# A gated ConvFFN in four token groups: down tiles issued between the next group's up blocks

## What is computed

```python
def conv_ffn(h, past, w_up, w_conv, b_conv, w_down):
    up = h @ w_up
    full = jnp.concatenate([past.astype(up.dtype), up], axis=1)
    conv = b_conv + full[:, 0:t] * w_conv[0]
    for k in range(1, CONV_W):
        conv = conv + full[:, k:k + t] * w_conv[k]
    gate, val = jnp.split(conv, 2, axis=-1)
    return (jax.nn.gelu(gate) * val) @ w_down, full[:, t:]
...
    x = x + gate_f * f
...
y_prompt = rms_norm(xp, final_g)
```

## Time and profile before

| | us |
|---|---|
| median of 2 runs | 1898.5 (1896.73 to 1900.27) |
| the profiled execution | 1895.18 |
| its span, slowest of 8 cores | 1893.5 |
| span of the other cores | 1873.4 to 1892.7 |
| TensorE busy over the span | 61% |
| VectorE, ScalarE, GpSimd busy | 49%, 32%, 27% |
| granted TensorE clock, mean | 0.828 on this core |

### The profile page before, as it was taken

The page is one execution under the profiler, slowest core; times in us unless marked ns, Lnnn a source line. Parts: engine busy times, 40 slices in busy tenths (PEclk is TensorE's granted clock), DMA queues, the critical chain, the costliest instruction groups (busy, mean ns, idle before and its releaser), DMA issues.

```text
span 1893.5 us, 26226 instructions; the slowest of 8 cores (1873.4 to 1893.5 us)
## 1 busy us (share of the span) xinstructions
PE 1147.3 (61%) x6276; PEld 584.0 (31%) x6276; DVE 920.6 (49%) x2237; ACT 610.8 (32%) x1104; POOL 513.6 (27%) x464
## 2 busy tenths in 40 slices
PE   0020554236244318659999885789897577886493
PEld 0020443123122103324444442333343233333241
DVE  0057516741555404534444364778623588885031
ACT  0010003651144406733333253445412244442012
POOL 0056511120000003431110363555412244442011
PEclk9999955558566658979999797999998788898797
DMA  6155982322300170044431774997523244448922
GB/s 26 20 53 51 94 177 90 123 67 82 91 23 23 15 72 4 1 45 40 37 30 14 156 212 90 121 115 69 54 84 95 23 45 46 46 48 21 34 99 84
DMA packets 269959, 124.08 MB, mean 66 GB/s; under 512 B 234145, under 2 KB 256161, under 8 KB 268946
## 3 DMA queue, kind: packets, MB, share of 16 engines
q0 software_dynamic: 187344, 54.01, 29.0%
q1 hardware_dynamic: 82466, 68.39, 17.8%
HBM read 147.78 MB, written 28.60 MB: 93 GB/s over the span
## 4 chain that ended last, share of the span: by engine, by line
PE 36%; DMA 19%; DVE 14%; issue 11%; ACT 9%; SPq 5%; POOL 4%; DVEq 0%; POOLq 0%; ACTq 0%
PE pb L1164 12%; DMA x1t<-x_scratch 5%; SPq L106 5%; PE pb L668 3%; PE pb L659 3%; DMA wdn<-w_down 3%; DMA wad<-w_ada 2%; POOL yt L1263 2%; PE pb L708 2%; PE pb L564 2%; ACT hT L428 2%; PE pb L482 2%; PE pb L662 2%; PE pb L671 2%; PE pb L665 2%
## 5 line engine op out<-in xcount | busy, mean ns | idle before, releaser
L1164 PE MATMUL pb<-hT,wug 128*128 128x512 bf16 (+1 forms) x880 | 199.7, 374 | 107.5 <-DVE carry L1181 32.9
L1164 PE MATMUL pb<-hT,wuv 128*128 128x512 bf16 (+1 forms) x880 | 190.9, 362 | 14.8 <-DVE Cg L1188 7.3
L1256 PE MATMUL pb<-wdn,aT 128*128 128x512 bf16 x748 | 168.0, 388 | 43.0 <-DVE yt L1261 28.6
L1211 POOL TENSOR_TENSOR aT<-Gg,Cv 128x512 bf16<-128x512 f32 (+1 forms) x110 | 124.7, 1134 | 231.5 <-DVE Cv L1200 72.1
L1164 PEld LDWEIGHTS pb<-hT,wug 128*128 128x128 bf16 x880 | 81.7, 103 | 211.4 <-issue 143.0
L1164 PEld LDWEIGHTS pb<-hT,wuv 128*128 128x128 bf16 x880 | 82.0, 102 | 113.5 <-issue 42.8
L1256 PEld LDWEIGHTS pb<-wdn,aT 128*128 128x128 bf16 x748 | 74.0, 100 | 136.7 <-issue 53.3
L317 PE MATMUL pb<-cT,wad 128*128 128x17 bf16 x384 | 36.9, 183 | 120.7 <-DMA wad<-w_ada 90.2
L1175 ACT ACTIVATE Cv<-pb,bcv,wc 128x512 f32<-128x512 f32 x88 | 68.7, 780 | 122.6 <-PE pb L1164 56.5
L1263 POOL TENSOR_TENSOR yt<-yt,x1t 128x1024 f32<-128x1024 f32 x17 | 39.8, 2342 | 186.3 <-DMA x1t<-x_scratch 175.9
L1175 ACT ACTIVATE Cg<-pb,bcv,wc 128x512 f32<-128x512 f32 x88 | 68.7, 781 | 63.1 <-PE pb L1164 59.8
(11 more groups left out here) (288 smaller groups left out, 2438.7 us busy)
## 6 DMA issues: line engine op xcount, KB each, us to landing
wad<-w_ada POOLq DMA_DIRECT2D x48, 256.0 KB, 5.6
wug<-w_up POOLq DMA_DIRECT2D x44, 256.0 KB, 4.7
wuv<-w_up POOLq DMA_DIRECT2D x44, 256.0 KB, 5.6
xt<-x SPq DMA_DIRECT2D x17, 512.0 KB, 4.8
xtB<-x SPq DMA_DIRECT2D x17, 512.0 KB, 5.8
x_scratch<-x1r SPq DMA_DIRECT2D x17, 512.0 KB, 3.9
x1t<-x_scratch SPq DMA_DIRECT2D x17, 512.0 KB, 4.0
y<-yt SPq DMA_DIRECT2D x17, 512.0 KB, 2.9
```

Source lines behind the costliest of these rows:

```text
L1164: P.op("pe", lambda e, k=k, bank=bank, wsl=wsl: e.matmul(pb[bank][:, 0:tn], wsl[:, k, :], h2T[:, k, t0:t0 + tn], start=(k == 0), stop=(k = ...
L1211: P.op("pool", lambda e: e.tensor_tensor(aT[:, i, t0 - a0:t0 - a0 + tn], G[:, 0:tn], Cvt[:, 0:tn], ALU.mult), reads=[Gk, "Cv%d" % par], wr ...
L1256: P.op("pe", lambda e, kc=kc, h=h, loc=loc, bank=bank: e.matmul(pb[bank][:], aT[:, kc, loc:loc + 128], wdn[:, kc, h * 512:(h + 1) * 512], ...
```

## The change

The groups become `[[0], [1], [2], [3, 4]]`. A down tile is now a function, `down_tile`. At the end of a group its tiles go to a list, `pending`, and are issued during the next group's up stage, one after every 4th block (every 8th in the last group); what remains comes after the last group. `aT` becomes two buffers of 640 rows. w_down's pieces are issued during the first group, as before, but with one block per slice between them. The output staging `cv_so` is gone, and `Gg` is used for it.

```diff
-        aT = mk(ph, "aT", [128, 22, 1152], BF16)
+        aTs = [mk(ph, "aT%d" % i, [128, 22, 640], BF16) for i in range(2)]
...
-        groups = [[0, 1], [2, 3, 4]]
+        groups = [[0], [1], [2], [3, 4]]
...
-                if n < 2 * 22 and 2 <= i < 10 and bi == 0:
+                if n < 22 and 2 <= i < 10 and bi == 0:
                     load_wdn(i - 2)
...
+        def down_tile(t, loc, ab, abk):
+            par = ntile[0] % 2
+            ntile[0] += 1
...
+        pending = []
         for gidx, grp in enumerate(groups):
             a0 = TBS[grp[0]][0]
+            ab = aTs[gidx % 2]; abk = "aT%d" % (gidx % 2)
...
             LAG = 1
+            every = max(1, len(items) // (len(pending) + 1)) if pending else 0
             for step in range(len(items) + LAG):
                 if step < len(items):
                     up_s1(items[step])
                 if step >= LAG:
                     up_s2(items[step - LAG])
-            if stop_after == "F1":
-                return
+                if pending and step > 0 and step % every == 0:
+                    down_tile(*pending.pop(0))
+            while pending:
+                down_tile(*pending.pop(0))
             if gidx + 1 < len(groups):
                 load_up(0, nload % NW); nload += 1
...
+                    pending.append((t0 // 128 + tt_, t0 - a0 + tt_ * 128, ab, abk))
+        while pending:
+            down_tile(*pending.pop(0))
+
+        so = [Gg[0], Gg[1]]
```

More of the change, by code:

```diff
@@ L1204, in up_s2 @@
         def up_s2(item):
-            i, bi, slot, first_load, a0, n = item
+            i, bi, slot, first_load, a0, n, ab, abk = item
             par = n % 2
@@ L1210, in up_s2 @@
             P.op("act", lambda e: e.activation(G[:, 0:tn], Cgt[:, 0:tn], AF.Gelu_apprx_tanh), reads=["Cg%d" % par], writes=[Gk])
-            P.op("pool", lambda e: e.tensor_tensor(aT[:, i, t0 - a0:t0 - a0 + tn], G[:, 0:tn], Cvt[:, 0:tn], ALU.mult),
-                 reads=[Gk, "Cv%d" % par], writes=["aT"])
+            P.op("pool", lambda e: e.tensor_tensor(ab[:, i, t0 - a0:t0 - a0 + tn], G[:, 0:tn], Cvt[:, 0:tn], ALU.mult),
+                 reads=[Gk, "Cv%d" % par], writes=[abk])
         nblk = 0
-        ntile = 0
+        ntile = [0]
@@ L1216, in ffn_phase @@
         if stop_after == "F0":
             return
+        def down_tile(t, loc, ab, abk):
+            par = ntile[0] % 2
+            ntile[0] += 1
+            x1 = x1t[par]; x1k = "x1t%d" % par
+            P.dma("sp", x1[:], dr["x1"][t * 128:(t + 1) * 128, :], reads=["x1_d%d" % t], writes=[x1k])
+            dbanks = (4, 5) if par == 0 else (6, 7)
+            for h in range(2):
+                bank = dbanks[h]
+                for kc in range(22):
+                    P.op("pe", lambda e, kc=kc, h=h, bank=bank: e.matmul(pb[bank][:], ab[:, kc, loc:loc + 128], wdn[:, kc, h * 512:(h + 1) * 512], start=(kc == 0), stop=(kc == 21)),
+                         reads=[abk, "wdn"], writes=["pb%d" % bank])
+            y = yt[par]; yk = "yt%d" % par
+            g = gf_p if t < 16 else gf_s
+            for h in range(2):
+                P.op("dve", lambda e, h=h: e.tensor_tensor(y[:, h * 512:(h + 1) * 512], pb[dbanks[h]][:], g[:, h * 512:(h + 1) * 512], ALU.mult),
+                     reads=["pb%d" % dbanks[h], "gf_p", "gf_s"], writes=[yk])
+            P.op("pool", lambda e: e.tensor_tensor(y[:], y[:], x1[:], ALU.add), reads=[yk, x1k], writes=[yk])
+            ss = rs_all[:, 2 * NT + t: 2 * NT + t + 1]
+            ssk = "F_ss%d" % t
+            P.op("act", lambda e: e.activation(junk[:], y[:], AF.Square, accum_out=ss), reads=[yk], writes=["junk", ssk])
+            P.op("dve", lambda e: e.tensor_scalar(ss, ss, 1.0 / D, EPS, ALU.mult, ALU.add), reads=[ssk], writes=[ssk])
+            P.op("act", lambda e: e.activation(ss, ss, AF.Sqrt), reads=[ssk], writes=[ssk])
+            P.op("dve", lambda e: e.reciprocal(ss, ss), reads=[ssk], writes=[ssk])
+            P.op("dve", lambda e: e.scalar_tensor_tensor(y[:], y[:], ss, fg_bc[:], ALU.mult, ALU.mult), reads=[yk, ssk, "fg_bc"], writes=[yk])
+            P.dma("sp", dr["y"][t * 128:(t + 1) * 128, :], y[:], reads=[yk])
@@ L1245, in ffn_phase @@
                 for tt_ in range(tn // 128):
[L1246 to L1269, removed]
@@ L1279, in ffn_phase @@
                 c0 = c - 3
-                sx = so[(c // 4) % 2]; sk = "cv_so%d" % ((c // 4) % 2)
-                P.op("act", lambda e, sx=sx, bank=bank: e.copy(sx[:], pb[bank][0:32, :]), reads=["pb%d" % bank], writes=[sk])
-                P.dma("sp", dr["scvo"][:, c0 * 128:(c0 + 4) * 128], sx[:], reads=[sk])
+                sx = so[(c // 4) % 2]; sk = "Gg%d" % ((c // 4) % 2)
+                P.op("act", lambda e, sx=sx, bank=bank: e.copy(sx[0:32, :], pb[bank][0:32, :]), reads=["pb%d" % bank], writes=[sk])
+                P.dma("sp", dr["scvo"][:, c0 * 128:(c0 + 4) * 128], sx[0:32, :], reads=[sk])
 _NC_CACHE = {}
```

7 lines of the change are left out of this document (2 added, 5 removed).

## The result

| | before | after |
|---|---|---|
| median, same chip | 1901.3 us (10 runs) | 2134.5 us (11 runs) |
| ratio | | 1.1197 [1.1157, 1.1237] |
| profiled execution, its span | 1895.2, 1893.5 | 2140.8, 2139.2 |
| TensorE, VectorE, ScalarE, GpSimd busy | 61, 49, 32, 27% | 56, 43, 30, 28% |

The change costs 12.0%. 2085 us had been predicted, 9.8% over before, in a range from 1985 to 2165: sign, size and mechanism held. In some executions the cores of one die run at a lower granted clock and take some per cent longer; the ratios leave these out, and so do the times of the experiments.

What follows compares the result with a forecast made beforehand. No engine is full; in one-block groups the weight loads' round trip with two slots was taken to set the pace. 1170 + 173 + 384 + 233 + 120 = 2080 us of span, forecast 2085 us, range 1985 to 2165.

Steps and rivals of the forecast that it cites:

- What bounds it: Up groups: 8.5 us from the end of a weight slice's last block to the start of the slice two further on.
- not slower: Rival: loads run ahead of need, tiles fill TensorE's gaps, only the DMA engines bind; 1872 us; chance 0.06.
- Ordinary block: Up-projection block with one weight pair per block: 6.5 us taken, between 6.0 at full clock and 7.7 at half.
- first group: First 22 up blocks with w_down's 8 pieces among them, until the next group's first matmul: 173 us.
- Can't go faster than 5.4 us per block: Groups with one block per weight pair: a pair costs 5.4 us of all 16 DMA engines, so no block is faster.
- rivals' sums: Totals of rivals: quick loads, high clock 2020 us (0.25); clock falls in every pause 2180 (0.17); loads hide 1872 (0.06).
- A long burst ahead leaves the clock alone: TensorE's clock: a 2.5 us pause halves it, but a 0.76 us pause or a long burst ahead does not.
- Cycle of the middle groups: Second and third group: four up blocks and one down tile take 36.5 us; each group 192 us.
- Table loads: ScalarE, two per tile at 1.28 us each, 24 more; the skill's 1.38 us drain per switch (33 us) left out.
- Fourth group: 22 full and 22 short blocks at 7.5 us per slice, 165, plus four tiles at 17, 68: 233 us.
- The stall that goes: GpSimd's first multiply of the second up group: 22 us of waits on 352 aT-reading matmuls disappear.
- Tail: Last down tiles: four fewer at 10.89 us, 163.5 to 120 us; p_conv stores and the x1 load behind them stay.

## Why the prediction was right, step by step

- **What bounds it.** Right. The latency from a block's end to the matmuls two slices on, read from one load in the earlier trace rows, decides: a third slot, with loads that run on across the borders, removes some 170 of the 233 us by which the kernel became slower, and so does leaving the reloads out.
- **The slot for "not slower".** The prediction named its condition, a third weight buffer or less than 3.5 us from issue to start. With the buffer the time is 1959, not the 1872 of that rival, so the condition was needed and not sufficient: a tile in the last group costs 15 us, not the 12 in all that the rival had for four of them, and middle groups take 4 blocks and a tile in 32 us, not 22.
- **Ordinary block and first group.** 6.9 a block against 6.5, within its bounds of 6.0 and 7.7, and 180 us against 173. The clock is the reason for the block's: neither high nor low throughout, but low at the start of each pair. TensorE waits for weights at every second block, not at nearly every one. The group's 7 us have another reason beside it: the first ten blocks took 88 us where the sum has 93, the last twelve 83 where it has 70, which is less than twelve of its own 6.5 (78).
- **"Can't go faster than 5.4 us per block".** Wrong, though only rivals' sums rest on it: with three slots and no tiles between, a block takes 4.9. The price of a pair in the earlier trace rows, a share of time in a stretch that wasn't full, is no lower bound.
- **"A long burst ahead leaves the clock alone".** The earlier trace rows doesn't show it, and the rows after speak against it for pauses of this length. Here a tile and a block had run ahead of the pause, and the set takes 3.52 us all the same, where one at full clock takes 1.9:

```profile
1402.35 3.52 PE L1164 MATMUL pb<-hT,wug 128*128 128x512 bf16 x8 [5.28 <-DMA wug<-w_up]
```

- **Cycle of the middle groups.** Right, 35.8 to 36.8 in the second group, and with it the steps behind a tile: the second, third and fourth block start 8.9, 17.8 and 22.9 us behind its matmuls (1393.45), where 8.8, 16.8 and 23 had been worked out. The third group's one pitch of 41.5 makes the 5 us there.
- **Table loads.** 1.28 us each, 22 more of ScalarE's instructions in all (24 had been said). The Trainium skill, "ScalarE: Activation LUTs", What ACT_TABLE_LOAD costs, has a further drain of about 1.38 us for each switch; the rows after show 0.01 to 0.02 us, and the 33 us that it would have added were rightly left out.
- **Fourth group, the term that was mis-sized most.** I put the pace of a slice at VectorE's 7.5 us and wrote that this is "above the load chain's need" without working the chain out for a slice with a decode block. By the rows it is 3.2 us longer there (11.7 for 8.5), since GELU stands behind ScalarE's copies; with the slice that then runs (7.3, as 1768.53 to 1775.9) that is 19.0 for two. The term was 37 us too small for 22 slices and 6 us too large for four tiles (17 against 15.6), 31 in all. This is half of the 59 us that the sum was short; the rest are small terms, all of the same sign.
- **The stall that goes.** Right, and so is the reason, that the loads' own waits come first: without the loads the stall is back, in two parts. GpSimd, the first product into the reused buffer in the kernel after:

```profile
1565.05 1.26 POOL L1211 TENSOR_TENSOR aT<-Gg,Cv 128x512 bf16<-128x512 f32 x1 [3.75 <-ACT Gg L1210]
```

- **Tail.** Right, 124 against 120. SyncE's issue of `p_conv` stays, and GpSimd waits for the x1 load behind it:

```profile
2015.19 19.57 SPq L106 DMA_DIRECT2D p_conv<-cvo_p  x2
```

```profile
2072.69 2.34 POOL L1235 TENSOR_TENSOR yt<-yt,x1t 128x1024 f32<-128x1024 f32 x1 [52.30 <-DMA x1t<-x_scratch]
```

## What to carry to other kernels

Before making groups smaller, work out the time from the last use of a buffer slot to the first use of its next filling, every instruction between them in each queue included (8.5 us here, 11.7 where a decode block is in between), and compare it with the work that the other slots cover: fewer blocks per slice shrink the cover, and one more slot, with loads that run on from group to group, was worth some 170 us here. Do it for each kind of slice, not for the common one alone. And look at the plain stalls first: a redundant wait, an element-wise store and a load queued behind a store were a few lines each, and gave together what no order of the loops did.

## What the runs showed of the hardware

- A semaphore wait that is already met costs GpSimd 63 ns: 351 fewer took 21.95 us out of one stall, and 17 us out of the time (21 by the ratio). 176 of them stand in front of each of the two products that idled for 14.85 and 16.72 us when the loads were left out.
- Two stores of 5632 single elements each held SyncE's issue, together, for 15.5 us before and 19.6 after, and the x1 load behind them for longer: storing by rows put the next add 31.7 us earlier (1783.70 to 1751.95). They cost the whole kernel 36 us, for some 45 KB.
- After a pause of 4.6 to 4.8 us TensorE's first set of 8 matmuls ran at a granted clock of 0.50 (1.2 GHz), the second at 0.77 over the set, and the block behind them at 1.00 (2.4 GHz). So the granted clock of the first group, 0.78, is a mean of its two levels.
- Behind its table load of 1.28 us the root started after 0.02 us, GELU after 0.01.
